# A hybrid mLSTM and attention block on eight cores: each attention head's epilogue is issued inside the next head's loop

## What is computed

```python
def one_block(j):
    start = j * A_QBLOCK
    qb = lax.dynamic_slice_in_dim(q, start, A_QBLOCK, axis=3)
    logits = jnp.einsum('bhmqd,bhmkd->bhmqk', qb, k)
    dist = (start + jnp.arange(A_QBLOCK, dtype=jnp.int32))[:, None] - k_pos[None, :]
    bias = bias_tab[:, t5_bucket(dist)]
    logits = jnp.where(dist >= 0, logits + bias[None, :, None], -jnp.inf)
    p = jax.nn.softmax(logits, axis=-1)
    wts = p[:, :, 0] - lam * p[:, :, 1]
    return jnp.einsum('bhqk,bhkd->bhqd', wts, v)
...
ha = (rms_norm(ha, a_norm_g[l].reshape(A_HEADS, A_V_DIM)) * (1.0 - lam_init)).reshape(b_, s_, A_WIDTH).astype(x.dtype)
```

## Time and profile before

| | |
|---|---|
| median of 3 runs | 7129.51 us (7051.94 to 7176.56) |
| the profiled execution's own time | 7069.98 us |
| its span, slowest core (core 3) | 7068.4 us |
| spans of the 8 cores | 6959.1 to 7068.4 us |
| TensorE matmul busy | 4904.8 us, 69% |
| ScalarE busy | 3712.9 us, 53% |
| VectorE busy | 2554.5 us, 36% |
| GpSimd busy | 130.5 us, 2% |
| chain that ended last, by engine | TensorE 59%, ScalarE 13%, VectorE 10%, DMA 9%, issue 8% |

### The profile page before, as it was taken

How to read it: one execution, slowest core, us unless ns; L and a number is a source line. 1 busy time by engine, 2 the same in 40 slices (tenths; PEclk the granted TensorE clock), 3 DMA queues, 4 the chain that set the end, 5 groups by cost and what they waited for, 6 DMA issues and landing times.

```text
span 7068.4 us, 96859 instructions; the slowest of 8 cores (6959.1 to 7068.4 us)
## 1 busy us (share of the span) xinstructions
PE 4904.8 (69%) x30216; PEld 2603.7 (37%) x30216; DVE 2554.5 (36%) x5233; ACT 3712.9 (53%) x8056; POOL 130.5 (2%) x196
## 2 busy tenths in 40 slices
PE   8004555558677777867876886787678768876887
PEld 6002222233244335324433533443255335433543
DVE  0102333445433532542253245316331532253225
ACT  0113343445374467437546854775387458646864
POOL 0000000000000000000000000000000000000000
PEclk8555665667787788778988988898799879988998
DMA  5993122123111311312131131123212221222122
GB/s 182 251 260 137 54 79 78 57 100 104 61 42 66 146 45 41 140 57 61 69 140 58 43 137 70 58 67 117 81 46 79 105 84 48 73 110 85 48 74 99
DMA packets 141277, 645.25 MB, mean 91 GB/s; under 512 B 20720, under 2 KB 25328, under 8 KB 96112
## 3 DMA queue, kind: packets, MB, share of 16 engines
q1 hardware_dynamic: 125424, 571.82, 24.5%
q0 software_dynamic: 15360, 67.25, 2.7%
HBM read 571.76 MB, written 67.24 MB: 90 GB/s over the span
## 4 chain that ended last, share of the span: by engine, by line
PE 59%; ACT 13%; DVE 10%; DMA 9%; issue 8%; DVEq 0%; SPq 0%; ACTq 0%; POOL 0%; POOLq 0%
PE bank L924 12%; PE bank L940 9%; PE bank L1077 9%; PE bank L621 7%; PE bank L1121 5%; DMA wb_scr<-s_wbo 4%; PE bank L1004 4%; PE bank L559 2%; PE bank L1018 2%; PE bank L998 2%; PE bank L406 2%; ACT s_pex L930 2%; ACT s_njunk L488 1%; ACT s_hT L504 1%; PE bank L729 1%
## 5 line engine op out<-in xcount | busy, mean ns | idle before, releaser
L930 ACT ACTIVATE s_pex<-bank,s_farb 128x512 bf16<-128x512 f32 (+1 forms) x3128 | 1842.1, 804 | 320.6 <-PE bank L924 149.1
L924 PE MATMUL bank<-s_Qbd,s_kch 128*128 128x512 bf16 (+1 forms) x3392 | 1286.2, 384 | 177.9 <-DMA s_kch<-kt_scr 122.8
L940 PE MATMUL bank<-s_vch,s_pex 128*128 128x130 bf16 x12672 | 1303.3, 225 | 4.7 <-ACT s_pex L928 2.4
L940 PEld LDWEIGHTS bank<-s_vch,s_pex 128*128 128x128 bf16 x12672 | 1013.4, 100 | 405.2 <-issue 94.1
L499 PE MATMUL bank<-s_identb,s_n1xn 128*128 128x128 bf16 x512 | 64.7, 305 | 750.3 <-DMA s_xs<-x 390.9
L1077 PE MATMUL bank<-s_hT,s_pf 128*128 128x512 bf16 x2304 | 558.1, 407 | 37.3 <-DVE s_fu L1096 22.6
L1096 DVE SCALAR_TENSOR_TENSOR s_fu<-bank,s_fcw,s_fu 128x511 f32<-128x511 f32 (+1 forms) x704 | 493.4, 744 | 239.1 <-ACT s_fhalo L1089 163.4
L924 PEld LDWEIGHTS bank<-s_Qbd,s_kch 128*128 128x128 bf16 x3392 | 338.2, 100 | 484.3 <-issue 263.8
L1121 PE MATMUL bank<-s_w_down,s_actT 128*128 128x512 bf16 x1584 | 379.9, 407 | 135.9 <-DVE s_actT L1106 135.9
L1081 ACT ACTIVATE s_fu<-bank,s_fcb,s_fcw 128x510 f32<-128x510 f32 x352 | 286.2, 813 | 278.0 <-DVE s_actT L1106 213.7
L488 ACT ACTIVATE s_njunk<-s_xs 128x1024 bf16<-128x1024 f32 x100 | 106.5, 1065 | 554.9 <-DMA s_xs<-x 482.9
(11 more groups left out here) (216 smaller groups left out, 6402.2 us busy)
## 6 DMA issues: line engine op xcount, KB each, us to landing
s_pf<-wb_scr SPq DMA_DIRECT2D x120, 1024.0 KB, 11.9
s_wst<-wall SPq DMA_DIRECT2D x32, 2048.0 KB, 19.6
s_vch<-va_scr SPq DMA_DIRECT2D x208, 260.0 KB, 2.7
s_kch<-kt_scr SPq DMA_DIRECT2D x208, 256.0 KB, 2.8
s_w_down<-wb_scr SPq DMA_DIRECT2D x9, 5632.0 KB, 21.9
wb_scr<-s_wbo POOLq DMA_DIRECT2D x32, 1024.0 KB, 20.0
s_xs<-x SPq DMA_DIRECT2D x64, 512.0 KB, 5.8
s_wup<-wb_scr SPq DMA_DIRECT2D x27, 1024.0 KB, 7.1
```

The costliest lines, as they stand in the source:

```text
L924: S.op("pe", lambda e: e.matmul(sv, lhsT=kch[ri][:, kk * 128:(kk + 1) * 128], rhs=rhs, start=True, stop=not near), reads=[b_kch[ri], b_Qbd ...
L930: S.op("act", lambda e: e.activation(out=pex[px][:, 0:256 * nq], in_=sv, func=AF.Exp, bias=farb[:, h:h + 1], scale=1.0), reads=[spb, cb[14 ...
L940: S.op("pe", lambda e: e.matmul(ab[:, m * 130:(m + 1) * 130], lhsT=pex[px][:, c0:c0 + 128], rhs=vch[ri][:, kk, :], start=False, stop=False ...
```

## The change

The epilogue becomes a generator, `attn_epi`. Its first slice copies the four accumulators out of their banks into a new SBUF tile `accS`; it is issued right behind the head's last item. The other slices are the same operations as before, reading `accS` instead of the banks: one per query block, then Square, the reduce, logarithm with exponential, the four scalings, and last the transposes with the copy to `haT`. One slice is issued after every sixth item of the next head (the transposes after the 54th). What is left when that head ends is issued before its own copies, and behind the last head all of its slices are issued at once. The small tiles exist twice, by the parity of the head.

```diff
@@ -882,6 +882,52 @@
                             S.dma("sp", kch[ri][:, 0:nk * 128], kt_d[h_, :, s0 * 128:(s0 + nk) * 128], reads=[b_ktd], writes=[b_kch[ri]])
                             S.dma("sp", vch[ri][:, 0:nk, :], va_d[h_, :, s0 * 130:(s0 + nk) * 130].rearrange("p (b c) -> p b c", c=130), reads=[b_vad], writes=[b_vch[ri]])
 
+                        accS = [sbt(st, "accS%d" % i, [128, 4, 2, 130]) for i in range(2)]
+                        b_accS = [S.buf("accS%d" % i) for i in range(2)]
+                        rr2 = [sbt(st, "rr2_%d" % i, [128, 8]) for i in range(2)]
+                        har2 = [sbt(st, "har2_%d" % i, [128, 4, 128]) for i in range(2)]
+                        hsq2 = [sbt(st, "hsq2_%d" % i, [128, 4, 128]) for i in range(2)]
+                        hss2 = [sbt(st, "hss2_%d" % i, [128, 8]) for i in range(2)]
+                        haf2 = [sbt(st, "haf2_%d" % i, [128, 4, 128], BF16) for i in range(2)]
+                        b_ep = [S.buf("epi%d" % i) for i in range(2)]
+
+                        def attn_epi(h, accs):
+                            p = h % 2
+                            aS, rr, har, hsq, hss, haf, b_a = accS[p], rr2[p], har2[p], hsq2[p], hss2[p], haf2[p], b_ep[p]
+                            for jq in range(4):
+                                ab, abb = accs[jq]
+                                S.op("dve", lambda e: e.tensor_copy(out=aS[:, jq, :, :], in_=ab[:, 0:260].rearrange("p (m c) -> p m c", m=2)), reads=[abb], writes=[b_accS[p]])
+                            yield
+                            for jq in range(4):
+                                av = aS[:, jq, :, :]
+                                S.op("dve", lambda e: e.tensor_scalar(out=rr[:, 2 * jq:2 * jq + 2], in0=av[:, :, 128], scalar1=1e-30, scalar2=None, op0=ALU.max), reads=[b_accS[p]], writes=[b_a])
+                                S.op("dve", lambda e: e.reciprocal(out=rr[:, 2 * jq:2 * jq + 2], in_=rr[:, 2 * jq:2 * jq + 2]), reads=[b_a], writes=[b_a])
+                                S.op("dve", lambda e: e.tensor_tensor(out=rr[:, 2 * jq + 1:2 * jq + 2], in0=rr[:, 2 * jq + 1:2 * jq + 2], in1=neglam[:], op=ALU.mult),
+                                     reads=[b_a, CONST], writes=[b_a])
+                                S.op("dve", lambda e: e.tensor_scalar(out=har[:, jq, :], in0=av[:, 0, 0:128], scalar1=rr[:, 2 * jq:2 * jq + 1], scalar2=None, op0=ALU.mult),
+                                     reads=[b_accS[p], b_a], writes=[b_a])
+                                S.op("dve", lambda e: e.scalar_tensor_tensor(out=har[:, jq, :], in0=av[:, 1, 0:128], scalar=rr[:, 2 * jq + 1:2 * jq + 2], in1=har[:, jq, :],
+                                                                            op0=ALU.mult, op1=ALU.add), reads=[b_accS[p], b_a], writes=[b_a])
+                                yield
+                            S.op("act", lambda e: e.activation(out=hsq[:], in_=har[:], func=AF.Square, scale=1.0 / math.sqrt(128.0)), reads=[b_a], writes=[b_a])
+                            yield
+                            S.op("dve", lambda e: e.tensor_reduce(out=hss[:, 0:4], in_=hsq[:], axis=AX.X, op=ALU.add), reads=[b_a], writes=[b_a])
+                            yield
+                            S.op("act", lambda e: e.activation(out=hss[:, 4:8], in_=hss[:, 0:4], func=AF.Ln, bias=epst[:, 0:1], scale=1.0), reads=[b_a, CONST], writes=[b_a])
+                            S.op("act", lambda e: e.activation(out=hss[:, 4:8], in_=hss[:, 4:8], func=AF.Exp, scale=-0.5), reads=[b_a], writes=[b_a])
+                            yield
+                            for jq in range(4):
+                                S.op("dve", lambda e: e.scalar_tensor_tensor(out=haf[:, jq, :], in0=har[:, jq, :], scalar=hss[:, 4 + jq:5 + jq], in1=ang[:, h * 128:(h + 1) * 128],
+                                                                            op0=ALU.mult, op1=ALU.mult), reads=[b_a, CONST] + cb, writes=[b_a])
+                            yield
+                            tb, tbb = banks[4 + h % 3], bbufs[4 + h % 3]
+                            tv = bfview(tb)[:, 0:512].rearrange("p (j t) -> p j t", j=4)
+                            for jq in range(4):
+                                S.op("pe", lambda e: e.transpose(out=tv[:, jq, :], in_=haf[:, jq, :], identity=identb[:]), reads=[b_a, cb[0]], writes=[tbb])
+                            S.op("dve", lambda e: e.tensor_copy(out=haT[:, h, :], in_=tv.rearrange("p j t -> p (j t)")), reads=[tbb], writes=[b_haT])
+                            yield
+
+                        epi = [iter(())]
                         for h in range(4):
                             accs = [(banks[jq], bbufs[jq]) for jq in range(4)]
                             for jq in range(4):
@@ -948,29 +994,14 @@
                                 gcount[0] += 1
                                 if gcount[0] % MSTEP == 0:
                                     next(mdrv, None)
-                            for jq in range(4):
-                                ab, abb = accs[jq]
-                                av = ab[:, 0:260].rearrange("p (m c) -> p m c", m=2)
-                                S.op("dve", lambda e: e.tensor_scalar(out=rr[:, 2 * jq:2 * jq + 2], in0=av[:, :, 128], scalar1=1e-30, scalar2=None, op0=ALU.max), reads=[abb], writes=[b_a])
...
-                                                                            op0=ALU.mult, op1=ALU.add), reads=[abb, b_a], writes=[b_a])
...
-                            tv = bfview(tb)[:, 0:512].rearrange("p (j t) -> p j t", j=4)
-                            for jq in range(4):
-                                S.op("pe", lambda e: e.transpose(out=tv[:, jq, :], in_=haf[:, jq, :], identity=identb[:]), reads=[b_a, cb[0]], writes=[tbb])
-                            S.op("dve", lambda e: e.tensor_copy(out=haT[:, h, :], in_=tv.rearrange("p j t -> p (j t)")), reads=[tbb], writes=[b_haT])
+                                if idx % 6 == 5:
+                                    next(epi[0], None)
+                            for _ in epi[0]:
+                                pass
+                            epi[0] = attn_epi(h, accs)
+                            next(epi[0], None)
+                        for _ in epi[0]:
+                            pass
                         for _ in mdrv:
                             pass
                         S.barrier()
```

More of the change, by code:

```diff
@@ L962, in build_program @@
[L962 to L965, removed]
@@ L966, in build_program @@
-                            for jq in range(4):
-                                S.op("dve", lambda e: e.scalar_tensor_tensor(out=haf[:, jq, :], in0=har[:, jq, :], scalar=hss[:, 4 + jq:5 + jq], in1=ang[:, h * 128:(h + 1) * 128],
-                                                                            op0=ALU.mult, op1=ALU.mult), reads=[b_a, CONST] + cb, writes=[b_a])
-                            tb, tbb = banks[4 + h % 3], bbufs[4 + h % 3]
-                            tv = bfview(tb)[:, 0:512].rearrange("p (j t) -> p j t", j=4)
```

## The result

In ten runs each, the changed kernel took 6868.43 us in the median (6822.94 to 6990.6), the kernel before 7093.65 (7008.96 to 7206.92). The ratio is 0.9748, 95% interval 0.970 to 0.980: 2.5% faster, about 178 us of 7070, where 191 (2.7%) were forecast. The medians are of all ten runs, while every ratio here leaves out the runs that a slower state of the chip disturbed.

A forecast was written before the change was run, and what follows sets the result against it. Inside heads ScalarE paces; at head boundaries only the epilogue does. Removed stops of 294 us, less 23, 8, 31 and 16, plus 20, less 29, 10 and 6, save 191 us; off 7129.5 that gives 6938, predicted as 6935, range 6835 to 7030.

The forecast's parts named there:

- the clock's term: After inner head boundaries, TensorE's granted clock no longer falls: 0.7 us each, 20 us gained, bounds 5 and 30.
- the 10 us of unit 7: Unit 7 has 35 steps per head, so only five slices fit; the remainder drains at boundaries: 10 us lost.
- its bounds: Unknown terms: transposes 0 to 1.7 per head, clock 5 to 30, late P·V 0 to 25, unit 7 and mLSTM 5 to 35.
- The inner gap: ScalarE's stop at 27 inner head boundaries: 294 us removed, about 0.85 us each staying, 23 us.
- the prediction's own sign: Profile after, at inner boundaries: 1 to 3 us between exponentials if the prediction is right.
- P·V behind the memsets: Next head's first P·V waits for copies and memsets where VectorE starts late: 8 us in all.
- In the loop: Inside heads: ScalarE's moved operations cost 31 us, transposes in score banks 16 (0.6 each), mLSTM steps 6; clock gains 20.
- The last heads: Nine units' last heads have nothing to hide behind; copies precede their exposed epilogue chain: 29 us lost.
- Rival 1: Square, reduce or transposes wait at a queue's head inside heads: 110 us saved, 7020; chance 0.12.
- Rival 2: Denser attention holds dense stages outside it at the lower clock longer: 130 us saved, 7000; chance 0.09.
- Rival 3: VectorE falls behind its slices, Square blocks ScalarE's queue inside heads: 88 us slower, 7215; chance 0.04.
- The rule that I set aside: Epilogue operations reading SBUF instead of PSUM save 62 cycles each: 7 us back on nine exposed chains; not counted.

The follow-up runs named there:

- last_direct: Changed kernel with each unit's last head reading its accumulators from the banks, without copies; ratio to the kernel before 0.9681.
- every3: Changed kernel with a slice issued after every third item instead of every sixth; ratio to the kernel before 0.9705.
- best: Changed kernel with last head read from banks, unit 7 slices every third step, transposes in bank 7 where free after mLSTM; ratio to the kernel before 0.9656.
- every1: Changed kernel with a slice issued after every item instead of every sixth; ratio to the kernel before 0.9961.
- the first group: Follow-up runs of the control, copy_inline, last_direct and best, sharing their runs of the kernel before; ratios 0.9753, 1.0127, 0.9681 and 0.9656.
- copy_inline: Changed kernel with copies to SBUF kept but all epilogue slices issued at once at the head's end; ratio to the kernel before 1.0127.
- the control: The changed kernel run again, unedited, beside the follow-up kernels; ratio to the kernel before 0.9753.

## Why the prediction was right

The mechanism held: the stop at the inner boundaries went, the chain did not stall inside the heads, and the last heads lost what the copies cost. The net size held too, 178 us by the ratio and 186 to 193 by the stages against 191. That it came so close is partly luck, since the clock's term was about twice too large and the 10 us of unit 7 reappear in two other terms. The level was off: 6935 us forecast, 6868 measured. The base was the median of three runs, 7129.5, and the median of ten was 7094. The range also does not follow from its bounds: as listed they allow a saving of 110 to 236, not 125 to 235, and the spread of the runs was added only in part (6835 to 7030 in place of 6817 to 7052 with the prediction's own saving). The measured time lies inside either way. Point by point:

- **The inner gap.** Forecast: 294 us of stop before, 31 after (23 and 8). Measured: 303.1 and 36.6. In units 8 to 15 a typical stop is 0.74 to 0.91 (the prediction's own sign, 1 to 3 us, was too long). The excess over forecast is unit 7, whose second and third boundary keep 6.1 and 4.7 us, and one of 4.35 in unit 8 (core 0), where mLSTM's matmuls stand on TensorE ahead of the next head's scores and wait 1.15 us for ScalarE's L770.
- **P·V behind the memsets** where VectorE is late: TensorE waits 3.6 us in all for L934 in the changed kernel, where 8 us of stop were counted. The term is small.
- **In the loop.** Gaps fell by 266.5 and attention by 219 to 226, so the moved work and all else in the heads cost 41 to 48 net. Forecast were 31 for ScalarE's operations, 16 for the transposes and 6 for mLSTM, less 20 for the clock, 33. The difference is for the most part the clock's term (below). The transposes were under-sized: by the distance of exponentials around them they cost 0.7 us in bank 5, 0.9 to 1.0 in bank 6, and up to 1.2 in bank 4, where mLSTM's operations stand among them, against 0.6 forecast. Measured the same way, Square cost 0.50 us in the middle of its values, less than the 0.63 counted, and logarithm with exponential 0.70, more than the 0.51: in sum 1.2 against 1.14. No activation-table load came with the move, as forecast: the trace has 68 of them before and after, none of them in attention.
- **The last heads.** Forecast 29, with a share of unit 7's 10 on top; measured 33.5, of which unit 7 has 9.2. last_direct shows 25.7 of it to be the copies.
- **Unit 7.** Its attention still got 15 us shorter and its end 9.2 longer; with three items per slice attention falls by 9 more and the end by 4.3 (every3), or by 6.8 with the last head direct as well (best).
- **Rival 1** (waits inside heads) did not occur, and every1 shows what keeps it out.
- **Rival 2** (the clock takes some back) did not show in the stages outside attention. The first profile of the changed kernel has die 0 at 0.803 and die 1 at 0.836, and its rest is 4519.5 against 4516.5 before. Cleaner is the pair in the first group: copy_inline, with all its stops, has a rest of 4464.2 (both dies at 0.825), the control, without them, 4454.5 (0.842). But the argument against it, that attention itself is indifferent to the clock, held only before the change. In the changed kernel's first profile, attention of units 8 to 15 took 2080.5 us on die 0 and 2068.3 on die 1; before the change, 2279.4 (0.802) and 2276.8 (0.823). So at the lower clock the denser attention took up to 12 us more; the control, at 0.842 on both dies, has 2068.0 and 2066.6.
- **Rival 3** (slower) was right as a mechanism, wrong for this spacing; every1 is a spacing at which it nearly wipes the gain out.
- **The clock term.** The granted clock no longer falls at the inner boundaries of units 8 to 15: in the 8.9 us that follow a head's last P·V it was 0.56 to 0.81 before, and in the control 1.00 at 22 of the 24 and 0.81 at two (core 0). The first 24 exponentials behind these boundaries took 10.0 us less in sum in the control than before, 0.4 us per boundary, and the first 24 of a unit, ahead of which nothing changed, took the same. The prediction took 0.7 each: its own reading of one boundary, 0.3, was nearer, and the longer cold stretches that it assumed elsewhere did not come. Other changes at a head's start would be in the 0.4 too.
- **The rule that I set aside was half right.** I compared L958, a TENSOR_SCALAR, with L967, a SCALAR_TENSOR_TENSOR, and gave nothing for reading SBUF. The like pair is L958 and its successor: 350 ns out of a bank, 286 ns out of `accS`, 64 ns less. That agrees with the 62 cycles of the Trainium skill (VectorE: DVE Perf Modes, TRN2 errata), and also with its tier table, which lets an fp32 `tensor_scalar` run faster from SBUF alone. But the 62 cycles are a fixed cost and should show in every operation that read a bank before. They do not: L909 took 351 ns where L960 took 350, and the two-column L903 took 161 where L954 took 150. So these rows fit the tier table better, in which two columns leave nothing to speed up; it has no row for SCALAR_TENSOR_TENSOR. What was gained is 0.26 us per exposed chain, 2 us in all, where the prediction's estimate by the rule was 7.

## What to carry to other kernels

Moving a serial epilogue under the next iteration paid nearly the whole gap here only when its slices were spaced wider than the work in them and in the loop's own operations on every engine they touch; issued too densely, the same chain stalled the loop from the head of a queue. The last iteration has nothing to hide under: give it the short path, without the copy that the others need. And a moved step that borrows a buffer of the loop's own ring can cost the loop a bubble each time, here 0.7 to 1.0 us, so look for a buffer that is idle by then.

## What the runs showed of the hardware

- On core 0 before the change the exponentials kept their pitch at granted clocks of 1.00 and 0.81 (0.591 and 0.585 us), and attention agrees within 0.4% over cores whose mean clocks are 0.800 and 0.825. With the stops gone, attention of units 8 to 15 was 0.6% longer on the die at 0.803 than on the one at 0.836. The rest of the program before the change differs by 110 us between cores (4459 to 4569), the longer ones on the die at 0.802.
- A TENSOR_SCALAR of 128x128 fp32 took 350 ns from a bank and 286 ns from SBUF; a SCALAR_TENSOR_TENSOR took 350 and 351.
